# Two fused transformer blocks on one core: norms spread by transposes, an output projection begun between head norms, squares added in pairs

## The reference

```python
def first_block(x, mem, ...):
    for l in range(2):
        h = _rms(x, mix_norm_g[l])
        if l == 0: x = x + _even_mixer(h, ...)   # retention heads 0-3, HGRN2 heads 4-7
        else:      x = x + _odd_mixer(h, ...)    # dilated attention, 8 heads, q and k normed per head
        x = x + _memory_cross_attention(_rms(x, ...), _rms(mem, ...), ...)
        x = x + _conv_ffn(_rms(x, ffn_norm_g[l]), ...)
    return x

def _even_mixer(h, w_in, ret_norm_g, hg_norm_g, lb, w_out):
    rq, rk, rv, rg, gq, gf, gi, gg = _split_cols(h @ w_in, EV_SIZES)
    ret = _merge_heads(_head_layer_norm(ret, ret_norm_g)) * silu(rg)
    hg = _merge_heads(_head_rms_norm(hg, hg_norm_g)) * silu(gg)
    return concatenate([ret, hg], axis=-1) @ w_out          # 1024 -> 1024

def _memory_cross_attention(h, mem_h, w_q, w_kv, q_norm_g, k_norm_g, w_o):
    q = _rms(_split_heads(h @ w_q, 4), q_norm_g)            # 4 heads of 256 channels
    mk, mv = _split_cols(mem_h @ w_kv, (1024, 1024))        # 256 memory tokens
    mk = _rms(_split_heads(mk, 4), k_norm_g)
    p = softmax(einsum('bhqd,bhkd->bhqk', q, mk) * 256 ** -0.5)
    return _merge_heads(einsum('bhqk,bhkd->bhqd', p, mv)) @ w_o

def second_block(x, ...):                                   # two equal layers
    proj = rmsnorm(x, g) @ w_in                             # q, k, v, forget, conv, pool, gates
    x = x + (gated sum of forgetting attention (8 heads of 64, q and k normed), short conv, pooling) @ w_o
    x = x + (silu(h @ w_gate) * (h @ w_up)) @ w_ffn_out     # h = rmsnorm(x)
```

## Time and profile before

| | us |
|---|---|
| median of three runs | 3233.85 (3233.09 to 3234.19) |
| the profiled execution | 3237.08 |
| its span (first to last instruction) | 3235.3 |
| PE busy | 3151.6 (97%) |
| DVE busy | 1610.9 (50%) |
| ACT busy | 1075.6 (33%) |
| POOL busy | 282.8 (9%) |
| mean granted TensorE clock | 0.987 |

### The profile page before, as it was taken

How to read it: one execution, slowest core, us unless ns; L and a number is a source line. 1 busy time by engine, 2 the same in 40 slices (tenths; PEclk the granted TensorE clock), 3 DMA queues, 4 the chain that set the end, 5 groups by cost and what they waited for, 6 DMA issues and landing times.

```text
span 3235.3 us, 38949 instructions
## 1 busy us (share of the span) xinstructions
PE 3151.6 (97%) x15546; PEld 2615.3 (81%) x15546; DVE 1610.9 (50%) x1977; ACT 1075.6 (33%) x1165; POOL 282.8 (9%) x161
## 2 busy tenths in 40 slices
PE   8889999999999899999999999999999999999999
PEld 7767988888888798888888777888888777888887
DVE  7365544554334654455535755444433674544433
ACT  3222333443221442344422332333322342233322
POOL 0001200111001010001100200101100120101100
PEclk9999999999999999999999999999999999999999
DMA  4411321222231132122223222222233212222233
GB/s 165 123 40 40 117 92 52 96 99 104 104 117 68 51 108 101 53 91 91 104 104 97 80 79 91 93 103 91 95 105 107 88 59 102 99 96 91 91 105 116
DMA packets 47723, 299.94 MB, mean 93 GB/s; under 512 B 7091, under 2 KB 7347, under 8 KB 13284
## 3 DMA queue, kind: packets, MB, share of 16 engines
q1 hardware_dynamic: 42480, 288.01, 25.2%
q10 hardware_dynamic: 5108, 10.02, 1.3%
HBM read 293.26 MB, written 4.75 MB: 92 GB/s over the span
## 4 chain that ended last, share of the span: by engine, by line
PE 87%; DVE 6%; ACT 2%; issue 2%; DMA 1%; another core or an unknown queue 0%; POOL 0%; DVEq 0%; ACTq 0%; SPq 0%
PE G L436 79%; DVE wL L1526 1%; ACT wH L1113 1%; PE psT L517 1%; PE psS L718 1%; DMA raw<-in_units 1%; DVE ws L2196 1%; PE psS L895 1%; PE psS L492 1%; DVE mxt L1728 1%; PE G L902 1%; DVE ws L2193 0%; PE psS L996 0%; PE G L1005 0%
## 5 line engine op out<-in xcount | busy, mean ns | idle before, releaser
L436 PE MATMUL G<-hH,wH 128*128 128x512 f32 x2560 | 1017.6, 398 | 36.9 <-DVE wL L1526 11.0
L436 PE MATMUL G<-hL,wH 128*128 128x512 f32 x2560 | 1001.0, 391 | 0.0
L436 PE MATMUL G<-hH,wL 128*128 128x512 f32 x2560 | 1000.7, 391 | 0.0
L1526 DVE TENSOR_TENSOR wL<-raw,wH 128x2048 fp32r<-128x2048 f32 x265 | 637.6, 2406 | 645.2 <-ACT wH L1113 644.9
L436 PE MATMUL G<-wsr,wH 128*128 128x512 f32 (+1 forms) x2528 | 751.8, 381 | 1.4 <-DVE wsr L2069 0.9
L1113 ACT ACTIVATE wH<-raw 128x2048 fp32r<-128x2048 f32 x265 | 505.5, 1908 | 613.7 <-PE G L436 573.7
L436 PEld LDWEIGHTS G<-hH,wH 128*128 128x128 f32 x2560 | 483.7, 189 | 154.3 <-issue 28.9
L436 PEld LDWEIGHTS G<-hH,wL 128*128 128x128 f32 x2560 | 483.1, 189 | 102.7
L436 PEld LDWEIGHTS G<-hL,wH 128*128 128x128 f32 x2560 | 483.8, 189 | 100.1 <-issue 2.7
L436 PEld LDWEIGHTS G<-wsr,wH 128*128 128x128 f32 x2528 | 466.8, 189 | 95.2 <-DVE wsr L2069 1.8
L436 PE MATMUL G<-wsr,wL 128*128 128x512 f32 (+1 forms) x1264 | 479.1, 379 | 0.0
(11 more groups left out here) (267 smaller groups left out, 2633.4 us busy)
## 6 DMA issues: line engine op xcount, KB each, us to landing
raw<-in_units SPq DMA_DIRECT2D x265, 1024.0 KB, 4.8
ws<-bias_rows SPq DMA_DIRECT2D x2, 1536.0 KB, 14.8
bias_rows<-ws ACTq DMA_DIRECT2D x1, 2560.0 KB
x<-in_x SPq DMA_DIRECT2D x4, 512.0 KB, 7.8
ws<-in_mem ACTq DMA_DIRECT2D x2, 1024.0 KB, 5.0
ws<-bias_rows ACTq DMA_DIRECT2D x1, 2048.0 KB, 8.2
out_x<-x SPq DMA_DIRECT2D x4, 512.0 KB, 7.8
ws<-in_decay ACTq DMA_DIRECT2D x1, 1280.0 KB, 6.6
```

What stands on the lines that cost most here:

```text
L436: mm = pe.matmul(o, mv if swap else wt, wt if swap else mv, start=first and n == 0, stop=last and n == 2)
L1526: V.tensor_tensor(wL[:, g.p, :], raw[:, g.p, :], wH[:, g.p, :].bitcast(F32), ALU.subtract)\
```

## The change

Five things are altered.

1. **Spread.** DVE no longer writes diagonals. It copies the columns themselves (128x4, or 128x2 for 256 tokens) into `wide`, and PE makes four (two) transposes of a column that is read as broadcast over 128 free elements, with the identity. For the 64-channel heads DVE writes eight columns, each repeated 64 times (128x512), and four transposes make the whole tile in the place of two half spreads.
2. **HGRN2 head norms.** The output projection's k 0 to 3 of jobs 0 and 1 are put between the statistics and the four spreads; k 4 to 7 of job 0, the memory's statistics and k 4 to 7 of job 1 follow.
3. **Cross attention.** DVE adds the squares of a head's two tiles (`add_pair`), and PE's statistics of the four key heads and of the first three query heads take half the matmuls, waiting for `pair_ready` and not `sq_ready`.
4. **Start.** PE runs 16 matmuls of 128x128 on constants before its first job, and ACT an activation on a constant, ahead of its wait for x.
5. **Bias sums.** `bs` moves to rows 35 and 36 of the workspace, and the two waits for `bias_out` in the input projection go; one comes in before DVE reads job `GG`, in the HGRN2 part.

```diff
-        bs = ws[0:8, 29:31, :].rearrange("p a b -> p (a b)")[:, 0:E_W]
+        bs = ws[0:8, 35:37, :].rearrange("p a b -> p (a b)")[:, 0:E_W]
...
-            def stats(kind, m, ntt=ST, npairs=4, st=st):
+            def stats(kind, m, ntt=ST, npairs=4, st=st, added=None):
...
-                pe.wait_ge(sq_ready, c.sq.v + 1)
+                if added is None:
+                    pe.wait_ge(sq_ready, c.sq.v + 1)
+                else:
+                    pe.wait_ge(pair_ready, added)
                 for tt in range(ntt):
-                    for t in range(2):
+                    for t in range(2 if added is None else 1):
...
-            def spread(w=S, lo=0, hi=P, bank=None, o=None):
-                pe.wait_ge(diag_ready, c.bc.v + 1)
-                pe.matmul(psT[lo:hi, c.bc.p if bank is None else bank, 0:w] if o is None else o, ones[:, lo:hi],
-                          diag[:, c.bc.p, 0:w], start=True, stop=True).then_inc(rb_ready, 1)
+            def spread(w=S, o=None, pair=False):
+                pe.wait_ge(cols_ready, c.bc.v + 1)
+                if o is None:
+                    o = psT[:, c.bc.p, :]
+                for tt in range(w // P):
+                    if pair:
+                        col = wide[:, c.bc.p, tt * P:tt * P + P]
+                    else:
+                        col = wide[:, c.bc.p, tt:tt + 1].to_broadcast([P, P])
+                    mm = pe.transpose(o[:, tt * P:tt * P + P], col, ident[:])
+                mm.then_inc(rb_ready, 1)
                 c.bc.off += 1
...
             pe.wait_ge(consts, 5)
+            for n in range(16):
+                pe.matmul(psT[:, 1, 0:P], ident[:], ones[:], start=True, stop=True)
...
-                    for h in range(4):
-                        spread()
-                    residual(h_op, mem=True, operand=normed)
+                    out_part(0, range(4))
+                    spread()
+                    out_part(1, range(0, 2))
+                    spread()
+                    out_part(1, range(2, 4))
+                    spread()
+                    spread()
+                    residual(h_op, mem=True, begun=(lambda: out_end(0), lambda: out_end(1)))
...
                     if 1 <= j <= 4:
-                        stats("pair", j - 1, ntt=2)
+                        stats("pair", j - 1, ntt=2, added=7 * l + j)
...
                     if j:
-                        stats("pair", j - 1)
+                        stats("pair", j - 1, added=7 * l + 4 + j)
...
+            act.wait_ge(consts, 5)
+            activation(rden[:, 0:1], neghalf[:], ACT.Identity)
             act.wait_ge(g_in, 16)
...
-                        elif j == 8:
-                            act.wait_ge(bias_out, 16)
...
-            def diagonal(cols):
+            def columns(first, n=ST):
                 wait(dve, rb_ready, c.bc.v - 1)
-                for tt, col in enumerate(cols):
-                    ins = V.tensor_scalar(diag[:, c.bc.p, tt * P:tt * P + P], ident[:], rsb[:, col:col + 1], None, ALU.mult)
-                ins.then_inc(diag_ready, 1)
+                V.tensor_copy(wide[:, c.bc.p, 0:n], rsb[:, first:first + n]).then_inc(cols_ready, 1)
                 c.bc.off += 1
+            def column_pairs(first):
+                wait(dve, rb_ready, c.bc.v - 1)
+                V.tensor_copy(wide[:, c.bc.p, :].rearrange("p (n c) -> p n c", c=64),
+                              rsb[:, first:first + 8].unsqueeze(2).to_broadcast([P, 8, 64])).then_inc(cols_ready, 1)
...
-                        elif j == 7:
-                            dve.wait_ge(bias_out, 16)
...
                         if lev == 5:
+                            dve.wait_ge(bias_out, 16)
                             step(by_rb(GG))
...
+                def add_pair(j, w):
+                    dve.wait_ge(sq_ready, c.sq.v + j + 1)
+                    s2 = sq[:, (c.sq.off + j) % 2]
+                    V.tensor_tensor(s2[:, 0, 0:w], s2[:, 0, 0:w], s2[:, 1, 0:w], ALU.add).then_inc(pair_ready, 1)
...
                                    lambda g: g[:, 0, :].rearrange("p (b c) -> p b c", c=256)))
+                    if j < 4:
+                        add_pair(j, M)
...
                     step(squared(j, queries))
+                    if j < 3:
+                        add_pair(j, S)
```

More of the change, by code:

```diff
@@ L356, in col2 @@
             return pc[:, o:o + n]
-        LAYER = dict(job=JOBS_2, unit=UNITS_2, sq=12, stat=6, bc=10, row=32, rw=16, sm=2, hd=FT // 2, piece=8,
+        LAYER = dict(job=JOBS_2, unit=UNITS_2, sq=12, stat=6, bc=6, row=32, rw=16, sm=2, hd=FT // 2, piece=8,
                      lay=1, ar=14, mg=8, mh=4, pv=4)
@@ L429, in end_job, with passes @@
                 c.job.off += 1
-            def passes(o, w0, w1, op, k, cols, first, last, swap=False):
-                u = c.unit.p
+            def passes(o, w0, w1, op, k, cols, first, last, swap=False, u=None):
+                u = c.unit.p if u is None else u
                 for n, (w, h) in enumerate(((wH, op[0]), (wH, op[1]), (wL, op[0]))):
@@ L488, in stats @@
                             col = m * ntt + tt
-                            mm = pe.matmul(st[:, col:col + 1], lhs, ones[:, 0:1], start=(t == 0), stop=(t == 1))
+                            mm = pe.matmul(st[:, col:col + 1], lhs, ones[:, 0:1], start=(t == 0),
+                                           stop=(t == 1 or added is not None))
                         elif kind == "tile":
@@ L754, in _, with out_part, out_end @@
                         stats("tile", m, npairs=2)
-                    for h in range(4):
-                        spread()
-                    residual(h_op, mem=True, operand=normed)
+                    job0, unit0 = c.job.off, c.unit.off
+                    def out_part(n, ks):
+                        for k in ks:
+                            if k == 0:
+                                pe.wait_ge(wl_ready, unit0 + n + 1)
+                                pe.wait_ge(job_free, job0 + n + 1)
+                            normed(k)
+                            for t in range(2):
+                                w0 = k * 256 + t * P
+                                mm = passes(G[:, (job0 + n) % 2 * 2 + t, :], w0, w0 + P, h_op, k, slice(0, S),
+                                            k == 0, k == KT - 1, u=(unit0 + n) % 2)
+                        return mm
+                    def out_end(n):
+                        end_job(out_part(n, range(4, KT)))
+                        c.unit.off += 1
+                    out_part(0, range(4))
[6 more added lines that the diff above has]
+                    residual(h_op, mem=True, begun=(lambda: out_end(0), lambda: out_end(1)))
                     c.nrm.off += 8
@@ L935, in _ @@
                     if tt == 1:
-                        for b in range(2):
-                            spread(lo=64 * b, hi=64 * b + 64, bank=0)
+                        spread(o=psT[:, 0, :], pair=True)
                 end_job(mm)
                 c.unit.off += 1
-                for b in range(2):
-                    spread(lo=64 * b, hi=64 * b + 64, bank=1)
+                spread(o=psT[:, 1, :], pair=True)
                 def quarter(q):
@@ L972, in key_norm @@
                     pe.wait_ge(ms_ready, c.stat.v)
-                    for b in range(2):
-                        spread(lo=64 * b, hi=64 * b + 64, o=G[64 * b:64 * b + 64, 3, :])
+                    spread(o=G[:, 3, :], pair=True)
                 def fill(s_):
@@ L1691, in residual @@
                         rstd(4, 2, D)
-                        diagonal(range(2))
+                        columns(0, 2)
                     else:
@@ L1756, in ffn @@
                 rstd(4, ST, D)
-                diagonal(range(ST))
+                columns(0)
                 spread_rms()
@@ L1942, in head_norm @@
                         first = c.bc.off
-                        diagonal(range(4))
+                        columns(0)
                         for h in range(4):
                             if h < 3:
-                                diagonal(range(4 * h + 4, 4 * h + 8))
+                                columns(4 * h + 4)
                             dve.wait_ge(rb_ready, c.bc.v - (1 if h < 3 else 0))
@@ L2028, in _ @@
                                 first = c.bc.off
-                                diagonal(range(4))
-                                diagonal(range(4, 8))
+                                columns(0)
+                                columns(4)
                             step(squared(j - 4, store(ws[:, OQ + 2 * (j - 4):OQ + 2 * (j - 4) + 2, :], mul=gqk[:, 0:1])))
@@ L2040, in _ @@
                                 for h in (2 * j - 8, 2 * j - 7):
-                                    diagonal(range(4 * h, 4 * h + 4))
+                                    columns(4 * h)
                             else:
@@ L2144, in _ @@
                 by_token(2)
-                diagonal(range(ST))
```

(2 more changed lines are left out.)

28 lines of the change are left out of this document (13 added, 15 removed).

## The result

The changed kernel takes 3207.95 us (median of four runs, 3204.10 to 3209.62) where the kernel before, run beside it, takes 3234.02 (3233.09 to 3237.96): a ratio of 0.9914, with a 95% interval of 0.990 to 0.9927. That is 26 us less; the forecast was 34 less, 3200, in a range of 3188 to 3216. The two profiled executions lie closer to the forecast: spans of 3235.3 and 3205.4, 29.9 apart.

A forecast was written before the change was run, and what follows sets the result against it. PE bounds the kernel, with 87% of the chain of waits and busy for 97%. Gains of 1.9 + 5.0 + 1.6 + 8.2 + 9.9 + 3.2 + 2.4 + 2.0 = 34.2 us take 3233.85 to 3200, range 3188 to 3216.

The forecast's parts named there:

- The pace of 0.13 apiece: All spreads: transposes in a row cost 0.13 us each, so a full spread takes 0.52, a gain of 0.4.
- the rival of transposes without overlap: All spreads: 152 transposes at 0.274 us cost 41.6 where spreads took 36.0; total 3216; chance 8%.
- the stall: All spreads: a transpose of a broadcast column stalls PE, making the kernel slower, 3258; chance 3%.
- The HGRN2 norm: HGRN2 head norms through output projection job 1: reordering and cheaper spreads gain 8.2 us (4 to 11).
- 24 matmuls start at once: Behind the HGRN2 statistics, at 294.67: 24 matmuls run without a wait, priced at 0.234 us apiece.
- The second block: Forgetting attention plus four of the six single spreads: a gain of 3.6 us.
- half of it: Forgetting attention: eight spread pairs save 4.5 us, but PE then stands for DVE; 2.0 counted (1 to 3.5).
- Cross attention: Both layers: halved statistics and cheaper spreads, less DVE's additions, gain 5.0 us per layer, 9.9 in all (7 to 12).
- the rival of key jobs bound by DVE: Cross attention: each of eight key jobs loses 0.42 us to DVE and ACT; total 3205; chance 12%.
- Bias rows: Input projection: without the bias DMA wait PE starts 4.0 us earlier, plus half the clock's 1.9; 5.0 (2.5 to 5.9).
- Start: Kernel start: matmuls on constants raise the clock for the first nine matmuls; gain 1.9 us (0 to 3.2).
- 1.9 goes: Kernel start: nine matmuls take 2.1 us and not 4.0, if the clock rises and the pause leaves it up.

The follow-up runs named there:

- hg_filled: Changed kernel with 12 of 24 matmuls moved between the two HGRN2 statistics and the memory's statistics behind job 1; 3200.0 us.
- again: The changed kernel run once more with nothing altered; 3206.1 us.
- spread_only: The kernel before with the new spreads and nothing else of the change that takes time; 3217.0 us.
- fox_back: Changed kernel with the old spreads (DVE diagonals, two half matmuls) in the forgetting attention of both layers; 3201.5 us.
- both: Changed kernel with the two HGRN2-place moves (12 matmuls between statistics, memory's statistics behind job 1) and the forgetting attention's old spreads; 3199.9 us.

## Why the prediction was right, and where its terms were not

*The spread.* The pace of 0.13 apiece was right (0.116 and 0.11 on the chain), and neither the rival of transposes without overlap nor the stall came. The term held what it said wherever PE is the bound: 3.6 in the dilated attention for 3.2.

*The HGRN2 norm* is one of the two terms that were mis-sized most: 8.2 forecast, 5.6 measured. The order of events was right: no idle time behind the statistics, job 0 before the memory, PE's wait for the memory's squares (1.37 for 2.8 forecast). Two steps failed. "24 matmuls start at once", at 0.234 apiece, took 7.20 and not 5.6, as the clock fell behind the statistics though PE had work; and the statistics of the memory took 5.75 and not 3.77, as the clock fell 1.4 us after their start, behind the wait. The forecast priced the clock only in job 1. Of the missing 2.6, the memory's statistics are 2.0 and their later start 0.7 (22.5 us behind the end of the HGRN2 statistics, for 21.7); the 1.6 of the 24 matmuls mostly shortened PE's wait for the memory. hg_filled shows that full pace can be had for them. What the term did not part is that 3.3 of the 5.6 come from the cheaper spreads and 2.3 from the order.

*The second block* is the other: 3.6 forecast, 0.5 measured. The step "half of it" priced PE's standing for DVE and put the clock there at nothing. Three half-speed stretches in each layer, where the kernel before had one, stand in the first profile and in `again`, so they are no accident of one execution. But what brings them and what removes them is not settled: spread_only, with the same spreads, has one in the first layer and three in the second; fox_back has none in the first, and `both`, with the same form, none there and three in the second.

*Cross attention* came out near its size (4.4 in each layer for 5.0, without the 1.7 of the clock in layer 1), with the price in another place: the additions delayed nothing in the key jobs, and 1.1 in layer 0 and 0.5 in layer 1 went into the wait ahead of the scores. The rival of key jobs bound by DVE is refuted by their interval of 6.20.

*Retention norm*: 1.3 for 1.6, once the clock's 1.7 is taken out of the row.

*Bias rows*: the wait as forecast, 3.9 of 4.0; the clock's part, of which I counted half, comes in some executions and not in others, as `again` shows.

*Start*: the sum was right by luck and its reason wrong. The step "1.9 goes" failed: at full speed PE came to the statistics and to the second unit's weights before these were ready, and waited; of 1.9 only 0.5 was left, and its condition, that the pause leaves the clock up, held in seven profiles of ten. The table load, for which I had taken nothing, made up for it in part, and three slow matmuls fewer for another part.

*The sum.* 34.2 forecast, 29.9 between the profiles, and 26 to 31 between medians, by which series of the kernel before is taken. Of the missing 8 us, 4.3 lie in the terms, as the two profiles show; the rest lies in which executions are compared: the median of three runs that the forecast started from, 3233.85, is 3 below what the longer series gave. The 29.9 itself holds 3.4 of the clock's at places that the change does not touch, against which stand some 1.6 lost to it at the bias rows. The range's low end, 3188, does not come out of the bounds that are named for it: with them the gain is 41.3 and the time about 3192.5.

## What to carry to other kernels

A kernel whose matrix engine is busy for 97% can still lose 1% to its clock: count the stretches at the lower level, and where each begins, before a gain of a few microseconds is believed. Work that is due anyway can be moved into such a place: with 12 matmuls between two statistics, and the memory's statistics behind job 1, a stretch of 63.0 us became 58.1. And take a part's worth from its own stretch of the trace: two parts worth 2.3 and 6.2 us there could each be taken out with no change in the total.

## What was not expected of the hardware

The same program after the same pause of 2.2 us ran on at full clock in one execution and at half in another (granted 1.00 and 0.68 over 5 us). During thirty-two statistics of one column each, issued back to back with no pause ahead of them, the granted clock fell to 0.50, and stayed there for 6.8 us, into the next job. And 152 transposes more made a kernel only 5.7 us longer by its span, in an execution with 27 us less at half clock.
